# Products with 256 tokens' high and low parts side by side in one matmul, and a second sum that ScalarE copies and VectorE adds

## The reference

```python
a = rmsnorm(x);  z = a @ w_in          # mq mk mv mi mf mo gq gk gv glr gg ga gb
hm = mlstm_scan(mq, mk, mv, ...);      hm = layernorm(hm) * sigmoid(mo)
hg = gla_scan(gq, gk, gv, la, ...);    hg = rmsnorm(hg) * silu(gg)
h = x + (sigmoid(ga) * (hm @ w_pa) + sigmoid(gb) * (hg @ w_pb)) @ w_o
uz = rmsnorm(h) @ w_up                 # gate and value, 2688 each
h = h + (silu(conv3(gate)) * value) @ w_down
h = h + sigmoid(rmsnorm(h) @ w_ple_gate) * (p @ w_ple_proj)
y = rmsnorm(h)
```

## Time and profile before

| | value |
|---|---|
| median of the runs | 1194.08 us |
| the profiled execution: its time | 1193.33 us |
| its span | 1191.2 us |
| TensorE matmul, weight load busy | 98%, 95% of the span |
| VectorE busy | 62% |
| ScalarE busy | 32% |
| matmuls | 9673, each with a weight load |
| mean granted clock of TensorE | 0.997 |

### The profile page before, as it was taken

One profiled execution on the slowest core, in us unless ns is written; L12 is line 12 of the kernel. 1 busy time (PEld: TensorE's weight loads), 2 busy tenths in 40 slices (PEclk: granted clock), 3 DMA queues, 4 the chain that ended last, 5 costly groups with the idle time before them and its releaser, 6 DMA issues.

```text
span 1191.2 us, 22613 instructions
## 1 busy us (share of the span) xinstructions
PE 1170.8 (98%) x9673; PEld 1133.3 (95%) x9673; DVE 733.5 (62%) x1317; ACT 376.4 (32%) x526; POOL 2.3 (0%) x7
## 2 busy tenths in 40 slices
PE   8999999999999999999999999999999999999996
PEld 7999899999999999999999999999999999999995
DVE  6855568675777655563565667666666653323677
ACT  6243332134343322233333223222222321111544
POOL 0000000000000000000000000000000000000000
PEclk9999999999999999999999999999999999999998
DMA  6342232412223366453443541121232133222222
GB/s 218 113 143 89 89 107 89 143 72 91 91 88 108 124 230 223 166 179 128 151 141 128 178 147 72 72 106 72 72 107 72 60 142 126 72 93 94 72 107 80
DMA packets 48963, 138.59 MB, mean 116 GB/s; under 512 B 5460, under 2 KB 25108, under 8 KB 39776
## 3 DMA queue, kind: packets, MB, share of 16 engines
q1 hardware_dynamic: 16392, 89.39, 21.5%
q10 hardware_dynamic: 32472, 47.77, 11.8%
HBM read 113.15 MB, written 23.81 MB: 115 GB/s over the span
## 4 chain that ended last, share of the span: by engine, by line
PE 87%; DVE 6%; issue 4%; ACT 3%; DMA 1%; ACTq 0%; POOL 0%; DVEq 0%; POOLq 0%
PE ps L758 59%; PE ps L764 8%; PE ps L867 6%; PE ps L873 3%; PE ps L785 2%; DVE wlo L1136 1%; DMA xT<-in_xT 1%; PE aux L1021 1%; PE aux L1091 1%; PE aux L983 1%; PE aux L1011 1%; DVE stg L1228 1%; PE aux L977 1%; PE aux L918 0%; DVE xl L1695 0%
## 5 line engine op out<-in xcount | busy, mean ns | idle before, releaser
L758 PE MATMUL ps<-ahi,whi 128*128 128x288 f32 x1536 | 332.1, 298 | 0.2 <-issue 0.2
L758 PE MATMUL ps<-alo,whi 128*128 128x288 f32 x1536 | 329.8, 296 | 0.0
L758 PEld LDWEIGHTS ps<-ahi,whi 128*128 128x128 f32 x1536 | 247.9, 189 | 4.3 <-issue 1.5
L758 PEld LDWEIGHTS ps<-alo,whi 128*128 128x128 f32 x1536 | 246.1, 188 | 0.0
L1136 DVE TENSOR_TENSOR wlo<-wraw,whi 128x2048 fp32r<-128x2048 f32 (+1 forms) x82 | 176.1, 2147 | 79.7 <-ACT whi L1862 75.5
L1862 ACT ACTIVATE whi<-wraw 128x2048 fp32r<-128x2048 f32 (+1 forms) x87 | 156.5, 1799 | 153.2 <-PE ps L758 104.3
L758 PE MATMUL ps<-ahi,wlo 128*128 128x288 f32 x800 | 171.3, 296 | 0.0
L758 PEld LDWEIGHTS ps<-ahi,wlo 128*128 128x128 f32 x800 | 128.8, 189 | 0.0
L764 PE MATMUL ps<-ahi,wlo 128*128 128x288 f32 x736 | 105.5, 296 | 0.0
L764 PEld LDWEIGHTS ps<-ahi,wlo 128*128 128x128 f32 x736 | 100.7, 189 | 0.0
L758 PE MATMUL ps<-aclo,whi 128*128 128x288 f32 x336 | 72.0, 296 | 0.0
(11 more groups left out here) (391 smaller groups left out, 1670.2 us busy)
## 6 DMA issues: line engine op xcount, KB each, us to landing
wraw<-in_w_in SPq DMA_DIRECT2D x31, 1024.0 KB, 4.9
wraw<-in_w_up SPq DMA_DIRECT2D x21, 1024.0 KB, 4.8
gate_scratch<-stg ACTq DMA_DIRECT2D x32, 288.0 KB, 3.0
gt<-gate_scratch ACTq DMA_DIRECT2D x32, 288.0 KB, 3.1
wraw<-in_w_pgate SPq DMA_DIRECT2D x6, 1024.0 KB, 4.7
wraw<-in_w_down SPq DMA_DIRECT2D x8, 704.0 KB, 4.0
wraw<-in_w_down SPq DMA_DIRECT2D x8, 640.0 KB, 3.8
out_C_s<-st ACTq DMA_DIRECT2D x16, 256.0 KB, 2.6
```

The costliest lines, as they stand in the source:

```text
L758: mm = nc.tensor.matmul(ps[:, t % 2, a, 0:HALF], w, x(k)[:, a * HALF:(a + 1) * HALF], start=f, stop=e)
```

## The change

The high and low parts of the activations get one tensor (`apair`, `acpair`: 2 x k x tokens), so that one access pattern can read 256 tokens' high parts and, behind them, the same tokens' low parts. For the kinds mk, gq, gk, mo, gg, ga, gb, gate, value and down a step now has five matmuls (`wide_product`): tokens 256 to 575 (320 columns) with high part, low part, and low weights, all into the second bank; tokens 0 to 255, high and low parts side by side (512 columns) with high weights over the whole first bank; and their high parts with low weights (256 columns) into its lower half. The first bank then holds two sums, which must be added. ScalarE copies the second one to SBUF (`wide`, one buffer); VectorE adds it to the first (`add_wide`). mq, pa, pb, wo, the small projection and the embedding's gate stay as they are, and so do mv and gv.

ScalarE's copy stands in its queue at the tile's place in `sched`. VectorE first handles the 320 columns, then waits for the copy, adds, waits for its own add, and multiplies the 256 columns in SBUF. The DMA of a stg tile waits for that product (`stg_ready`) where it waited for `tile_free`.

```diff
+            def wide_product(t, blocks, pair, s, start=True, stop=True, ready=None, mid={}, low_part=None):
+                low_half, rest = ps[:, t % 2, 0, 0:WIDE], ps[:, t % 2, 1, 0:T - WIDE]
+                side_by_side = ps[:, t % 2, 0, :].rearrange("p (e c) -> p e c", e=2)
+                for n, (col, k) in enumerate(blocks):
...
+                    nc.tensor.matmul(rest, wh, pair[:, 0, k, WIDE:], start=first, stop=False)
+                    nc.tensor.matmul(rest, wh, pair[:, 1, k, WIDE:], start=False, stop=False)
+                    nc.tensor.matmul(side_by_side, wh, pair[:, :, k, 0:WIDE], start=first, stop=False)
+                    if low_part:
+                        continue
+                    nc.tensor.matmul(rest, wl, pair[:, 0, k, WIDE:], start=False, stop=last)
+                    mm = nc.tensor.matmul(low_half, wl, pair[:, 0, k, 0:WIDE], start=False, stop=last)
...
+            def add_wide(dst, t, x=None):
+                ng["wide"] += 1
+                dve.wait_ge(wide_ready, ng["wide"])
+                if x is not None:
+                    link(V.tensor_tensor(wide[:, :], x, wide[:, :], ALU.add))
+                V.tensor_tensor(dst, ps[:, t % 2, 0, 0:WIDE], wide[:, :], ALU.add).then_inc(tile_free[t % 2], 1)
+                dve.wait_ge(tile_free[t % 2], t // 2 + 1)
+                dve.sem_inc(wide_used, 1)
...
+                    V.scalar_tensor_tensor(dst[:, WIDE:], ps[:, t % 2, 1, 0:T - WIDE], c, rs[:, WIDE:],
+                                           ALU.mult, ALU.mult)
+                    add_wide(dst[:, 0:WIDE], t)
+                    V.scalar_tensor_tensor(dst[:, 0:WIDE], dst[:, 0:WIDE], c, rs[:, 0:WIDE], ALU.mult, ALU.mult)\
+                        .then_inc(fm_ready, 1)
...
-                    V.tensor_tensor(two(stg[:, k % 2, :]), full, two(rs[:, :]), ALU.mult).then_inc(fr, 1)
+                    x = stg[:, k % 2, :]
+                    V.tensor_tensor(x[:, WIDE:], ps[:, t % 2, 1, 0:T - WIDE], rs[:, WIDE:], ALU.mult)
+                    add_wide(x[:, 0:WIDE], t)
+                    V.tensor_tensor(x[:, 0:WIDE], x[:, 0:WIDE], rs[:, 0:WIDE], ALU.mult).then_inc(stg_ready, 1)
...
-                    V.tensor_tensor(gbuf[:, 2:2 + HALF], p0[:, 0:HALF], rsv[:, 0:HALF], ALU.mult)
-                    V.tensor_tensor(gbuf[:, 2 + HALF:2 + TP], p1[:, 0:n1], rsv[:, HALF:TP], ALU.mult)
+                    V.tensor_tensor(gbuf[:, 2 + WIDE:2 + TP], rest[:, 0:TP - WIDE], rsv[:, WIDE:TP], ALU.mult)
...
+                    add_wide(gbuf[:, 2:2 + WIDE], t)
+                    link(V.tensor_tensor(gbuf[:, 2:2 + WIDE], gbuf[:, 2:2 + WIDE], rsv[:, 0:WIDE], ALU.mult))
...
-                    V.tensor_tensor(two(vrs[:, :]), full, two(rsv[:, :]), ALU.mult).then_inc(fr, 1)
+                    V.tensor_tensor(vrs[:, WIDE:], ps[:, t % 2, 1, 0:T - WIDE], rsv[:, WIDE:], ALU.mult)
+                    add_wide(vrs[:, 0:WIDE], t)
+                    V.tensor_tensor(vrs[:, 0:WIDE], vrs[:, 0:WIDE], rsv[:, 0:WIDE], ALU.mult)
...
-                    V.tensor_tensor(two(x), full, two(x), ALU.add).then_inc(fr, 1)
+                    V.tensor_tensor(x[:, WIDE:], ps[:, t % 2, 1, 0:T - WIDE], x[:, WIDE:], ALU.add)
+                    add_wide(x[:, 0:WIDE], t, x[:, 0:WIDE])
...
+                    if kind in WIDE_KINDS:
+                        act.wait_ge(tile_ready, t + 1)
+                        if ng["wide"]:
+                            act.wait_ge(wide_used, ng["wide"])
+                        ng["wide"] += 1
+                        A.activation(wide[:, :], ps[:, t % 2, 0, WIDE:], ACT.Copy).then_inc(wide_ready, 1)
...
-                            act.wait_ge(tile_free[tt % 2], tt // 2 + 1)
+                            act.wait_ge(stg_ready, k + 1)
```

More of the change, by code:

```diff
@@ L37 @@
 HALF = T // 2
+WIDE = 256
+WIDE_KINDS = ("mk", "gq", "gk", "mo", "gg", "ga", "gb", "gate", "val", "down")
 QT = 32
@@ L771, in product @@
                 return mm
+            def wide_product(t, blocks, pair, s, start=True, stop=True, ready=None, mid={}, low_part=None):
+                low_half, rest = ps[:, t % 2, 0, 0:WIDE], ps[:, t % 2, 1, 0:T - WIDE]
+                side_by_side = ps[:, t % 2, 0, :].rearrange("p (e c) -> p e c", e=2)
+                for n, (col, k) in enumerate(blocks):
+                    if n in mid:
+                        mid_stage(mid[n])
+                    for q, before in ready or ():
+                        pe.wait_ge(q, before + k + 1)
+                    first, last = start and n == 0, stop and n == len(blocks) - 1
+                    wh, wl = whi[:, s, col:col + P], wlo[:, s, col:col + P]
+                    nc.tensor.matmul(rest, wh, pair[:, 0, k, WIDE:], start=first, stop=False)
[5 more added lines that the diff above has]
+                    mm = nc.tensor.matmul(low_half, wl, pair[:, 0, k, 0:WIDE], start=False, stop=last)
+                if low_part:
+                    pe.wait_ge(split_lo, low_part)
+                    for n, (col, k) in enumerate(blocks):
+                        wl, last = wlo[:, s, col:col + P], n == len(blocks) - 1
+                        nc.tensor.matmul(rest, wl, pair[:, 0, k, WIDE:], start=False, stop=last)
+                        mm = nc.tensor.matmul(low_half, wl, pair[:, 0, k, 0:WIDE], start=False, stop=last)
+                if stop:
+                    mm.then_inc(tile_ready, 1)
+                return mm
             def span_product(t, place, s, low_part, ready=None, mid={}):
@@ L843, in _ @@
                         slot(t)
-                        product(t, [(b * P, b) for b in range(11)], rows_of(achi), rows_of(aclo), u % 2, stop=False,
+                        wide_product(t, [(b * P, b) for b in range(11)], acpair, u % 2, stop=False,
                                 ready=((ff_hi, 0), (ff_lo, 0)) if i == 0 else None).then_inc(half_done, 1)
@@ L876, in _ @@
                     elif kind == "down":
-                        product(t, [(b * P, 11 + b) for b in range(10)], rows_of(achi), rows_of(aclo), w, start=False,
+                        wide_product(t, [(b * P, 11 + b) for b in range(10)], acpair, w, start=False,
                                 ready=((ff_hi, 0), (ff_lo, 0)) if i == 1 else None)
@@ L889, in _ @@
                     else:
+                        if kind in WIDE_KINDS and kind != "up":
+                            wide_product(t, [(k * 2 * P + n * P, k) for k in range(KT)], apair, w,
+                                         low_part=u + 1 if n == 0 else None)
+                            continue
+                        if kind == "up":
+                            if n == 0:
+                                pe.wait_ge(split_lo, u + 1)
+                            wide_product(t, [(k * 2 * P + n * P, k) for k in range(KT)], apair, w,
+                                         ready=((c_hi, 0), (c_lo, 0)) if (i, n) == (0, 0) else None, mid=mid)
+                            if KT in mid:
+                                mid_stage(mid[KT])
+                            continue
                         hi, lo, ready = {
@@ L1129, in _ @@
             lv = 0
-            ng = {"gt": 0, "stg": 0, "tn": 0, "vs": 0}
+            ng = {"gt": 0, "stg": 0, "tn": 0, "vs": 0, "wide": 0}
             def lo_part(u):
```

38 lines of the change are left out of this document (19 added, 19 removed).

## The result

| | before | after |
|---|---|---|
| median of the runs | 1194.06 us (1193.49 to 1194.39) | 1206.39 us (1205.24 to 1208.04) |
| the profiled execution: its time | 1193.33 us | 1206.57 us |
| its span | 1191.2 us | 1204.8 us |
| TensorE, VectorE, ScalarE busy | 98%, 62%, 32% | 97%, 65%, 34% |
| matmuls | 9673 | 8817 |

The ratio is 1.0104, 95% interval 1.009 to 1.0118: the change makes the kernel 12.3 us slower. 5.5 us were forecast, and the range ended at 1206.0. The sign and the places of the loss were right. The gain per step was half of what the sum had.

What follows compares the result with a forecast made beforehand. TensorE, holding 87% of the chain that ended last, was taken to bound the kernel. New waits of 16.9 us against 11.4 of gain made +5.5 us, 1199.6 us as a median, range 1194.0 to 1206.0.

Steps and rivals of the forecast that it cites:

- TensorE's saving: All 856 steps: one fixed part of 13.3 ns saved in each, 800 to 786.7 ns, 11.4 us gross gain.
- Rival A: All 856 steps: the 512-column matmul hides its fixed part wholly, 26.7 ns a step, 22.8 us saved, 1188.2; chance 0.06.
- rival C: The 512-column matmul pays its fixed part twice, nothing is saved: +16.9, 1211.0 us (1208.9 with the page's 2.5 ns); chance 0.06.
- Evacuation: Tile hand-over on VectorE: 1.35 us instead of 0.68, +0.67 for each stg tile, +0.45 for mk, gq, gk.
- rival B: Hand-overs cost half of 0.67 or faster tiles slip into waits: GLA +2.0, in all +0.9, 1195.0 us; chance 0.14.
- 1. mk: mk tiles: copy behind ScalarE's weight conversion, first mv tile ends at 72.7 us, lateness +2.5 us.
- 2. gq, gk: mLSTM chunks: later hand-overs, a gap of some 2 us at the third gq tile, +2.6 us.
- 3. GLA: mo, gg tiles: three hand-overs in series in chunks 1 to 3, 38.0 us chunk to chunk, +5.0 us, the largest term.
- 4. ga, gb: ga, gb tiles: conversion ahead of the copy, L1005 2.9 us late, less the tiles' gain: +1.5 us.
- 5. ConvFFN: Gate and value tiles: VectorE's idle time covers the hand-overs, no stall, 336 steps gain 4.5 us.
- Rival D: ConvFFN: the loop of VectorE and ScalarE is 0.3 us longer a unit, +2.8, 1202.4 us; chance 0.12.
- 6. Down and small projection: Down-projection gains 2.2 us; its last tile hands over later, ahead of the small projection's copies, +0.6 us.

Runs made afterwards that it cites:

- the run with the products alone: Changed kernel's five matmuls a step with the evacuation of the kernel before, second sum left out of the result: 1190.68 us, ratio 0.9964.
- The row of equal matmuls: Changed kernel with twelve rows of 64 unused matmuls behind its last tile, most of one width a row: 512 columns took 226.7 to 227.3 ns each.
- the run with two instructions: Change in mo and gg alone, tiles evacuated by two VectorE products, without ScalarE copy or add, second sum left out: 1196.59 us, ratio 1.0019.

## Why the prediction was right or wrong

**TensorE's saving: wrong, and the main error.** The step that failed is "No row has 512 columns. One end: the fixed part is also 13.3 ns there, 226.7 ns, a step of 786.7 ns." The row of equal matmuls shows 226.7 to 227.3 ns, so the number was right for a 512-column matmul among its like. What had no row was its neighbourhood: next to 320 columns a pair costs 6.2 ns more, and in the tile the step takes 793.4, as two of 256 give 800.1. The saving is 6.6 ns a step, 5.6 us for 856 steps instead of 11.4, and of the mixers' 2.3 us among them nearly nothing reaches the end (the run with the products alone). I had named saving nothing and twice as bounds, but the range was drawn from the hand-overs and the ConvFFN loop: with the right term the forecast would have been 1199.6 + 5.7 = 1205.3, which left 0.7 us up to its end for all else that went wrong. Rival A and rival C are both out: neither 26.7 nor 0 ns. The Trainium skill (TensorE: Matmul & The Clock Gate, section Back-to-back issue gap) has 2.5 ns beside N/2.4. It gives that for isolated matmuls, which the prediction passed over, and for a stream of weight loads and matmuls it has about 131 ns at 512 columns. No row here agrees with either: 512 columns take 227.3 ns in a row of their own, each with its weight load, where the formula gives 215.8. Its result as a rival, 1208.9, lies closer to what was measured than the forecast, but by another mechanism.

**Evacuation: right.** +0.67 us for an stg tile was 0.62 (368.35 to 369.65 against 0.68). ScalarE's copy takes 377 ns on average, foreseen near 385. So rival B, hand-overs at half cost, is out; the run with two instructions shows what half would have given, +2.0 in GLA with the measured pace, where B put it at +2.0.

**1. mk: right.** First mv tile forecast to end at 72.7; TensorE waited 0.79 us for the mk tile's add and another 0.54 for low parts, ScalarE took the tile up at 72.60, and the stage added 2.7 (2.5). The order of ScalarE's stream was the cause.

**2. gq, gk: right.** +2.9 against +2.6, with the one gap at the third tile: 1.77 us. The copy ahead of the conversion takes it away.

**3. GLA: right.** Chunk to chunk 38.0 as forecast, 1.03 us idle at L1120 (about 1.2) and 1.41 at L1136 (over 1). 5.7 against 5.0, of which the missing pace of 16 tiles explains up to 0.8.

**4. ga, gb: the place right, the size not.** +4.6 against +1.5. L1050 did wait 2 us (1.97 against 0.82), and low parts of weights another 1.5. Two terms were wrong or missing. One is the pace, up to 0.9 for 16 tiles. The other is the clock, at which the sum had nothing. Granted clock by stretch in the changed kernel (after the busy times, PEclk is the third number from the end):

```profile
495.00:500.00 5.00, 3.03 (x32) 2.08 (x34) 3.30 (x9) 1.84 (x5) 0.00 (x0) 0.96 0.81 269
500.00:505.00 5.00, 5.00 (x39) 3.44 (x30) 3.96 (x5) 2.49 (x4) 0.00 (x0) 0.70 0.36 118
```

and in the run with 512 columns in one run, which has the same stall of 1.97 us at that place:

```profile
495.00:500.00 5.00, 3.03 (x24) 2.36 (x28) 3.91 (x11) 1.19 (x3) 0.00 (x0) 1.00 0.78 250
500.00:505.00 5.00, 5.00 (x53) 3.98 (x46) 3.21 (x5) 3.14 (x4) 0.00 (x0) 1.00 0.31 98
```

Behind the stall TensorE fell to its lower level of 1.2 GHz for part of these 5 us, did 39 matmuls instead of 53 in them, and the next tile ended 1.6 us later than in the other execution. That is part of the forecast's missing 3.1 us; some 0.6 stays unexplained. Of the six profiled executions that come to this place with a stall of 1.9 to 2.0 us, four show the fall; how many of the others had it isn't known.

**5. ConvFFN: no stall, right; the gain wrong,** -2.2 for -4.5, by the first term alone. Rival D is out: the unit takes 12.70 us, and even at 12.63 no bank is late.

**6. Down and small projection:** -1.1 for -2.2, again the first term; +0.66 for +0.6, and the run with the last tile as before shows its cause.

Put together for the profiled pair: forecast 16.9 of waits less 11.4 of gain. The lag of 13.15 and 5.6 of gain make 18.8 of waits, 17.2 without the clock's 1.6. The waits were nearly right as a sum; the gain and, in the profiled execution, the clock account for the error.

## What to carry to other kernels

Fewer instructions at the same work save only what a row shows for that width in that order: put a matmul width that the trace doesn't have into a few rows of its own, and beside its later neighbours, before a gain is built on it. A cheaper product that leaves its result in two parts moves work to the engine that hands tiles over; where that engine is in a chain (here three hand-overs in a chunk), each 0.3 us on one hand-over cost 0.7 to 0.9 us a chunk, while ConvFFN with 2.2 us of slack took it for nothing: apply such a change by stage. And when a second engine joins a hand-over, look at what stands ahead in its own stream: a 1.9-us conversion ahead of a 0.4-us copy cost several microseconds, and an exchange of the two gave back all of it in mk and half in gq.
